# Five orders in a two-block transformer kernel: the opening's banks and loads, conv's seventh unit, the last high part in finish, the low parts around the last down result, and GpSimd's low part among its scales

## What is computed

```python
# first block, for each of 2 layers
x = x + 0.5 * swiglu(rmsnorm(x, ffn1_norm), gate, up, down)      # F = 2816
x = x + concat(sliding_window, moba, dsa attention of rmsnorm(x) @ w_in) @ w_out
x = x + 0.5 * swiglu(rmsnorm(x, ffn2_norm), gate, up, down)
# then a final rmsnorm, and the second block
x = x + post_norm(diff_attention(pre_norm(x)))
x = x + post_norm(conv_ffn(pre_norm(x)))    # (x @ w_in), causal conv of width 3, gelu(gate) * val, @ w_out
x = x + post_norm(forgetting_attention(pre_norm(x), shared k, v, gates))
x = x + post_norm(conv_ffn(pre_norm(x)))
```

## Time and profile before

| | us |
|---|---|
| median of three runs | 3137.25 |
| the profiled execution | 3136.89 |
| its span in the profile | 3135.1 |
| TensorE busy | 3085.1 |
| VectorE busy | 2095.1 |
| ScalarE busy | 1372.0 |
| GpSimd busy | 821.9 |

### The profile page before, as it was taken

How to read it: one execution, slowest core, us unless ns; L and a number is a source line. 1 busy time by engine, 2 the same in 40 slices (tenths; PEclk the granted TensorE clock), 3 DMA queues, 4 the chain that set the end, 5 groups by cost and what they waited for, 6 DMA issues and landing times.

```text
span 3135.1 us, 47847 instructions
## 1 busy us (share of the span) xinstructions
PE 3085.1 (98%) x17664; PEld 2608.0 (83%) x17664; DVE 2095.1 (67%) x3335; ACT 1372.0 (44%) x2308; POOL 821.9 (26%) x627
## 2 busy tenths in 40 slices
PE   8999999999999999999999999999999999999999
PEld 6999876898989899777899977677888886778887
DVE  6869587685958586695867753556556546576474
ACT  5535246452535353354634433644334335343242
POOL 3212346521333133264412220240000332310003
PEclk9999999999999999999999999999999999999999
DMA  4355331333334433221343333123333231223232
GB/s 125 106 148 153 102 101 41 94 102 101 104 85 115 114 88 102 77 61 54 101 121 89 103 93 96 39 61 87 107 87 100 81 96 41 68 68 109 86 99 82
DMA packets 530032, 289.14 MB, mean 92 GB/s; under 512 B 13630, under 2 KB 520225, under 8 KB 529850
## 3 DMA queue, kind: packets, MB, share of 16 engines
q1 hardware_dynamic: 527162, 281.26, 31.4%
q0 software_dynamic: 2688, 5.44, 0.5%
HBM read 284.38 MB, written 10.02 MB: 94 GB/s over the span
## 4 chain that ended last, share of the span: by engine, by line
PE 84%; DVE 7%; issue 3%; ACT 3%; POOL 1%; SPq 1%; DMA 0%; DVEq 0%; ACTq 0%; POOLq 0%
PE bank L2373 38%; PE bank L2426 24%; PE bank L2391 5%; PE bank L2679 3%; PE bank L2789 2%; PE bank L2408 2%; PE bank L2476 2%; PE bank L2831 2%; PE bank L2854 1%; PE bank L2611 1%; PE bank L2517 1%; ACT w_hi L1009 1%; DVE w_lo L1612 1%; DVE h_lo L1642 1%; DVE scaled_g L1725 0%
## 5 line engine op out<-in xcount | busy, mean ns | idle before, releaser
L1009 ACT ACTIVATE w_hi<-w_raw 128x1024 fp32r<-128x1024 f32 (+1 forms) x319 | 367.6, 1152 | 1003.4 <-PE bank L2373 612.0
L1612 DVE TENSOR_TENSOR w_lo<-w_raw,w_hi 128x1024 fp32r<-128x1024 f32 (+2 forms) x287 | 420.1, 1464 | 254.8 <-ACT w_hi L1009 254.7
L2373 PE MATMUL bank<-h_hi,w_hi 128*128 128x512 f32 (+1 forms) x1204 | 476.7, 396 | 11.5 <-DVE h_lo L1642 4.5
L2373 PE MATMUL bank<-h_hi,w_lo 128*128 128x512 f32 (+1 forms) x1204 | 469.3, 390 | 0.0
L2373 PE MATMUL bank<-h_lo,w_hi 128*128 128x512 f32 (+1 forms) x1192 | 464.8, 390 | 0.0
L2426 PE MATMUL bank<-h_hi,ws 128*128 128x256 f32 x2432 | 452.7, 283 | 0.4 <-DVE ws L1796 0.4
L2426 PEld LDWEIGHTS bank<-h_hi,ws 128*128 128x128 f32 x2432 | 385.9, 192 | 1.4 <-DVE ws L1796 0.8
L2426 PE MATMUL bank<-h_lo,ws 128*128 128x256 f32 x1216 | 344.1, 283 | 0.0
L2426 PE MATMUL bank<-t_hi,ws 128*128 128x256 f32 x1824 | 341.1, 283 | 0.0
L2373 PE MATMUL bank<-act_hi,w_hi 128*128 128x512 f32 x836 | 325.3, 389 | 0.0
L2373 PE MATMUL bank<-act_hi,w_lo 128*128 128x512 f32 x836 | 325.2, 389 | 0.0
(11 more groups left out here) (390 smaller groups left out, 6245.6 us busy)
## 6 DMA issues: line engine op xcount, KB each, us to landing
w_raw<-in_ffn_w_down_dram SPq DMA_DIRECT2D x64, 704.0 KB, 4.7
w_raw<-in_ffn_w_in_dram SPq DMA_DIRECT2D x88, 512.0 KB, 3.8
raw_g<-in_ffn_w_gate_dram SPq DMA_DIRECT2D x76, 512.0 KB, 3.9
raw_u<-in_ffn_w_up_dram SPq DMA_DIRECT2D x67, 512.0 KB, 3.8
w_raw<-in_ffn_w_out_dram SPq DMA_DIRECT2D x32, 704.0 KB, 4.6
w_raw<-in_w_in_dram SPq DMA_DIRECT2D x34, 512.0 KB, 3.8
w_raw<-in_a_w_qkv_dram SPq DMA_DIRECT2D x24, 512.0 KB, 3.8
w_raw<-in_w_out_dram SPq DMA_DIRECT2D x16, 512.0 KB, 3.9
```

What stands on the lines that cost most here:

```text
L1009: nc.scalar.activation(split_home(c)[0][:, 0:nk, 0:cols], raw[c % 2][:, 0:nk, 0:cols], ACT.Copy).then_inc(hi_ready, 1)
L1612: nc.vector.tensor_tensor(w_low[:, 0:nk, 0:cols], raw[c % 2][:, 0:nk, 0:cols], w_high[:, 0:nk, 0:cols].bitcast(f32), ALU.subtract).then_in ...
L2373: mm = nc.tensor.matmul(result(c)[0:cols, :], w[:, k, 0:cols], x[k], start=(k == 0 and n == 0), stop=(k == nk - 1 and n == 2))
```

## The change

Five orders are changed; no instruction on data is added or removed.

- **Opening.** On SyncE the load of unit 3 and the first fast load of up weights move ahead of four small loads (lam_in). On ScalarE hi(3) moves from before the third full input to before the first. In the first stage alone, VectorE does gate_whole(1) directly behind lo(4) and product_whole(1) before lo(5), with the token low parts 0 and 1 behind act_low of product 1; ScalarE does silu 1, hi(5) and the second product's high part earlier, with token_high 1 and 2 behind them. product_whole(j) for j above 0 gets a wait for act_low of the product before.
- **Conv.** In the first half, three pairs instead of two are written out ahead of the loop. ScalarE's hi(at + 2) no longer waits for made_g, which ScalarE waits for behind it; VectorE does lo(at + 2) before the division in pair 2 of the first half.
- **finish.** hi(c + 2) moves behind the last half input.
- **output_gemm.** Five input low parts, not seven, stand ahead of the last take, and three behind it.
- **Mix.** GpSimd's low part moves from before pair_scale to between its first and its second phase.

```diff
@@ fast_ff (SyncE)
-                for u in range(3 if c == 0 else 0, 2 * FAST_FROM[0]):
+                for u in range(4 if c == 0 else 0, 2 * FAST_FROM[0]):
                     load(c + u, (gate, up)[u % 2][:, :, P * (u // 2):P * (u // 2 + 1)])
-                    if c == 0 and u == 3:
-                        fast_up(name, 0, FAST_FROM[0], up)
@@ the first loads (SyncE)
+            load(3, kview(A["ffn1_w_up"], 0)[:, :, P:2 * P])
+            fast_up(stages[0], 0, FAST_FROM[0], kview(A["ffn1_w_up"], 0))
             for n, w in enumerate(("a_lam_q1_2", "a_lam_k1_2", "a_lam_q2_2", "a_lam_k2_2")):
@@ pair_scale and its loop (GpSimd)
                 for u, ph in enumerate(plan["used"]):
+                    if u == 1 and unit is not None:
+                        low(unit)
                     if ph not in plan["pool"]:
                         continue
...
-                        if MIX_Q + p + lead(name) in POOL_LOW:
-                            low(BASE[name] + MIX_Q + p + lead(name))
-                        pair_scale(name, p)
+                        later = MIX_Q + p + lead(name)
+                        pair_scale(name, p, BASE[name] + later if later in POOL_LOW else None)
@@ finish (ScalarE)
                             half_root(following, 0)
-                        if half == 1 and k == 5:
-                            hi(c + 2)
+                hi(c + 2)
                 spread_copy(following, 0)
@@ full_input (ScalarE)
-                    if name == stages[0] and k == 2:
+                    if name == stages[0] and k == 0:
                         hi(3)
@@ gated_ff (ScalarE)
                         product_high(0, 0)
+                        silu(0, 1)
+                        hi(c + 5)
+                        product_high(0, 1)
                         if early:
                             token_high(name, 1)
-                            hi(c + 5)
-                        silu(0, 1)
-                        if early:
                             token_high(name, 2)
-                        else:
-                            hi(c + 5)
-                        product_high(0, 1)
@@ conv_ff (ScalarE)
-                    lead = 2 if hf == 0 else 1
+                    lead = 3 if hf == 0 else 1
...
-                        if early:
-                            act.wait_ge(*made_g)
-                        else:
-                            hi(at + 2, jj, also=made_g)
+                        if not early:
+                            hi(at + 2, jj)
+                        act.wait_ge(*made_g)
@@ output_gemm (VectorE)
-                    for k in range(KT - 1):
+                    for k in range(KT - 3):
                         h_low(follow, k)
                 take(c + KT - 1, KT - 1)
                 if follow:
-                    h_low(follow, KT - 1)
+                    for k in range(KT - 3, KT):
+                        h_low(follow, k)
@@ gated_ff (VectorE)
+                    if j:
+                        dve.wait_ge(act_ready, FF[name] + j)
                     nc.vector.tensor_tensor(prod[:, :], gated[:, :], result(c + 1)[:, :], ALU.mult).then_inc(bank_free[1], 1)
...
                         if early:
                             lo(c + 4)
+                            gate_whole(1)
                         product_whole(0)
                         if not early:
                             lo(c + 4)
                         act_low(a0 + 1, 0)
-                        gate_whole(1)
+                        if not early:
+                            gate_whole(1)
+                            token_low(name, 0)
+                        product_whole(1)
+                        lo(c + 5)
+                        act_low(a0 + 2, 1)
                         if early:
-                            lo(c + 5)
-                        token_low(name, 0)
-                        product_whole(1)
-                        if not early:
-                            lo(c + 5)
-                        act_low(a0 + 2, 1)
+                            token_low(name, 0)
                         token_low(name, 1)
@@ conv_ff (VectorE)
-                    lead = 2 if hf == 0 else 1
+                    lead = 3 if hf == 0 else 1
...
+                        sooner = hf == 0 and isinstance(j, int) and j == 2
+                        if sooner:
+                            lo(at + 2, jj)
                         divided(at, scaled_g[:, :], jj)
-                        if not early:
+                        if not early and not sooner:
                             lo(at + 2, jj)
-                        elif not first:
+                        elif early and not first:
                             lo(at + 3)
```

More of the change, by code:

```diff
@@ L884, in sub_diagonal, with pair_scale @@
                                         ALU.mult).then_inc(sub_diag, 1)
-            def pair_scale(stage, p):
+            def pair_scale(stage, p, unit=None):
                 plan = PLAN[stage, p]
                 for u, ph in enumerate(plan["used"]):
+                    if u == 1 and unit is not None:
+                        low(unit)
                     if ph not in plan["pool"]:
```

## The result

| | before | changed |
|---|---|---|
| median of six runs, us | 3137.18 | 3158.22 (3156.79 to 3159.69) |
| profiled execution, its span | 3135.1 | 3157.3 |
| mean granted clock | 0.998 | 0.995 |

The ratio is 1.0067, with an interval of 1.0054 to 1.008. The forecast was 3139.8 with a range up to 3146: the sign of the sum was right, its size was not; the worst case that the text worked out was 3149.7.

The account below looks back on a forecast made before the run. TensorE, busy 98% of the span, was taken as the bound, so each part was priced by its standing: −3.5 − 0.7 − 0 − 4.5 + 11.2 = +2.5, giving 3139.8 us against the median, range 3131 to 3146.

Parts of the forecast that it names:

- Opening, −3.5: Opening: fast pairs start 3.5 us sooner, from 1.6 idle time, 0.8 earlier high part and 1.1 shorter token low parts.
- its gain is bounded by its idle time: Opening, VectorE's chain before the fast pairs: operations all remain, so only idle time can go, 1.6 of 2.3 us.
- lose less: Opening: VectorE's token low parts lose less beside GpSimd, which ends 2 us sooner; 1.1 us gained.
- the full inputs and GpSimd's sums come 2.1 sooner: Opening: unit 3's load issued 2.4 us sooner, so ScalarE's last full input and GpSimd's token sums come about 2.1 sooner.
- Conv, −0.7: Conv's seventh unit and the loop's pace after it (0.1 × 7.5), less loss at the next unit: −0.35 in each of two stages.
- Half hand-overs, 0: Moving the last high part in finish behind two more half inputs changes nothing: 0, ends −0.6 and +0.3.
- Hand-overs, −4.5: Taking the last down result after five input low parts removes TensorE's gaps at the stage hand-overs: −4.5 us in sum.
- the low parts of blocks 5 and 6 come 0.6 later: Hand-over mix_0 to ffn2_0: these come 0.6 later, unnoticed by TensorE, the result and last low part 1.6 us sooner.
- Mix, +11.2: GpSimd's low part behind the first scales delays TensorE by slot (one pair's turn and a unit): 5.6 us per mix stage.
- Slots 2 and 6 change nothing: Mix: in these two slots the moved low part costs and gains nothing.
- slot 5's +0.6: Mix, slot 5: like slot 4, low part between the scale phases, but with shorter queues, costs 0.6 us per stage.
- rival 1: TensorE's stand in mix slot 0 lowers its clock, 1.6 us twice: 3143.0; slot 4 too 3146.2; opening too 3146.5–3149.7; chance 0.18.

Follow-up runs that it names:

- open_order: Kernel before with the opening's new order on VectorE and ScalarE but without its moved loads; 3138.52 us against 3136.93.
- t3_dve: raw_first with the first stage's fourth token sum made by VectorE behind the pair's sums instead of by GpSimd; 3136.55 us, 1.55 under raw_first.
- mix_busy: mix_only with 11 idle matmuls on TensorE ahead of slot 0's unit in each mix stage; median 3155.99 us, 0.8 under mix_only.
- conv_only: Kernel before with only the conv edits and the one in finish; 3135.16 us against 3136.93.
- mix_only: Kernel before with only the mix edit; 3156.76 us against 3137.56, ratio 1.0059.
- slot4_only: mix_only with GpSimd's low part between the scales in slot 4 alone, ahead of them in the other slots; 3142.84 us against 3137.43.
- raw_busy: raw_first with 12 idle matmuls on a free bank in TensorE's stand before the first pair's third product; 3137.42 us, 0.7 under raw_first.
- raw_first: open_order with the low part of the first pair's weights ahead of the token low parts on VectorE in the first stage; 3138.10 us against 3136.93.

## Why the prediction was right and wrong

The forecast of the sum missed by 18.4 us. By the account by part, 10.9 of it is the mix term, 5.4 the opening and 4.4 the hand-overs, less 1.2 in conv.

**Opening, −3.5, measured +2.25: two steps failed, "its gain is bounded by its idle time" with "lose less", and that the full inputs and GpSimd's sums come 2.1 sooner.** The idle time did go, 1.5 us of it. But the chain's own work got longer, by 1.3 where I had it 1.1 shorter: unit 5's low part, the activations' two and the first two token low parts took 9.7 us before (of which the earlier trace rows has 1.48 and 3.41) and 11.0 in the fence above with the 0.92 of the first activation. I had let all but the token low parts keep their durations. The idle time was no bound, because VectorE's own work did not set when the chain ended. A subtraction of two SBUF tensors that VectorE begins inside an addition or subtraction of GpSimd's ends a fixed time behind the end of that operation, whatever stood ahead of it; closing a gap in front of it makes it begin sooner and last longer. So the pairs start 4.0 us behind GpSimd's last operation: 53.47 and 57.48 before, 54.10 and 58.10 in the changed kernel, 53.34 and 57.35 in open_order. t3_dve shows it from the other side. The Trainium skill says in "GPSIMD Engine Reference", section 1 (Specifications), that GpSimd's SBUF interfaces are shared with VectorE and that there is contention with VectorE instructions that have two SBUF inputs; the trace agrees, for the products with a bank as an operand keep their 0.66 to 0.69 beside GpSimd, and those from SBUF alone grow.

GpSimd in turn started later, 38.24 for 37.42, and not 2.1 sooner. The load was issued at 23.73 instead of 25.12, not 2.4 us sooner: it waits for a low part of its own buffer (lo_ready), a condition that its old place had hidden. It landed 8.4 us later instead of 7.4 (what lengthened it isn't shown), at 32.1, so ScalarE stood 2.10 with all eight full inputs behind it instead of six, and the root came 0.8 later, where I had it 0.8 earlier. The 3 us before the pairs that the text gave as a condition for a lower clock became 4.4, and the clock fell (0.59 over 58 to 62): the pairs start 0.6 late and are 2.1 late when it is back.

Three readings of before's trace were off. TensorE's idle times add up to 44 us with the load, not 36. The lower clock behind unit 4's stand did not lose 1.6 us of the kernel's time: in mix_busy's execution, which has the opening of before, it stayed at 1.00 there and the pairs started at 57.45 for 57.48. And the clock fell a second time in that trace, behind a stand of half the length, near the end (the timeline, then the window):

```profile
3122.58 0.80 PE L2579 MATMUL bank<-rms,ones 128*128 128x256 f32 x2 [1.53 <-DVE rms L1681]
3122.00:3126.00 4.00, 3.42 (x16) 3.27 (x17) 3.01 (x7) 1.22 (x3) 2.47 (x4) 0.63 0.00 0
```

**Conv, −0.7, measured −1.8.** The mechanism was as worked out: the bank's evacuation is the new releaser. The first stand and what comes back at the next unit are together near the forecast in conv_0 (0.53 less, 0.34 given back) and worse in conv_1 (0.18 less, 0.38 given back). Mis-sized was the pace: I had 0.75 for each stage and took most of it as lost again; it gives 0.85 and 1.1, and keeps it.

**Half hand-overs, 0.** The order in finish moved the standing of conv_0's hand-over from one block to three (0.26, 0.25 and 0.18 in conv_only for 0.26 and 0.67), and not at all in the two others. It wasn't run alone; within conv_only it is under 0.3.

**Hand-overs, −4.5, measured +0.25: the step that "the low parts of blocks 5 and 6 come 0.6 later" and the last one 1.6 sooner failed.** It took 0.82 for each low part, the mean of a row that holds one of 1.79 beside GpSimd and six of 0.74. Behind the result GpSimd makes the square and the sum of squares, 3.1 us. The low part of block 6 begins inside the square and ends 0.55 behind it, at 602.77; that of block 7 begins inside the sum and ends 0.55 behind that, at 604.46: on before's time 0.7 later than there, not 1.6 sooner. With one or two low parts behind the result, none has to wait for the sum. The hint was in the same timeline: the one low part behind the result took 0.94, not 0.74. The ffn1 to mix hand-overs, for which I had a gain of 0.15, lost 0.4 each. The further 0.35 that I added for the first unit had no row.

**Mix, +11.2, measured +19.2: the terms "Slots 2 and 6 change nothing" and slot 5's +0.6 failed, and the clock, left out of the sum.** The mechanism and its main stands were right: 3.07 for 3.15 in slot 0, slot 1's 1.08 gone, 0.63 for 0.9 in slot 3, 1.65 for 2.0 in slot 4. Slot 2 was not nothing (a stand of 0.5 and 0.9 in the two stages, for the unit's low part) and slot 5 was 1.3 instead of 0.6: there too the second phase waits behind the low part. At full clock the part made 14.4 instead of 11.2, of which 12.7 are stands. The rest is rival 1, the clock: 4.8 by mix_only's median, 5.9 in its profiled execution, 7.7 in that of the changed kernel, where it fell five times in the mix stages. It had a chance of 0.18 against the row that spoke for it, 3.18 us in the opening with a clock of 0.90 behind, which was a stand of the same length as the forecast one; the forecast should have had the clock in its likeliest case, at 1.6 twice for slot 0. Slot 4's stand of 2.3 brought it as well. By the rule of the Trainium skill that the prediction cited ("TensorE: Matmul & The Clock Gate", Part 1: The HAM clock gate), that activity is what releases the throttle, a fall behind slot 0's stand was to be expected, and the traces agree.

## What to carry to other kernels

A duration read where two engines don't overlap isn't the price where they do, and a mean over a merged row can hide both. When an edit closes one engine's gaps or moves its work behind an event that starts the other, look up when the other's operations end in that stretch: here an operation that had to wait lasted until that end and a fixed time more. Closing a gap in front of it gains nothing; moving the neighbour's end does.

A low part or a scale that stands in idle time ahead of its user isn't in the way. Moving a whole loop's order for the one iteration in which it is (slot 1, 1.08 us) cost five others (slots 0, 2, 3, 4 and 5); decide by slot. And a new stand on TensorE of the length of one that already brings its clock down has to be priced with the clock.

## What the runs showed of the hardware

VectorE's 128x512 subtraction of two SBUF tensors took 0.69 us alone and 0.92, 1.48, 1.78 and 2.89 beside different operations of GpSimd. What looks like a factor is a wait. In the trace of before, each of the 167 subtractions of 128x1024 that VectorE began inside a TENSOR_TENSOR of GpSimd's, more than 0.14 us ahead of its end, ended 1.08 to 1.09 us behind that operation's end, and they lasted 1.28 to 3.41; alone they take 1.22. The 16 input low parts of 128x512 ended 0.55 behind it, and take 0.74 alone. The same times hold in all other traces, to 0.02 us. It goes the other way as well: GpSimd's sums of 128x1024 took 2.40 when they began first, and 2.8 to 3.4 when VectorE was at work, ending 2.2 to 2.3 behind the end of VectorE's operation.

TensorE's clock fell to 1.2 GHz at every one of the 15 stands of 2.9 us and more in the 18 profiled executions (the wait for x at the start aside), and behind stands of 1.06 and 1.25 (or 1.42 and 1.25) with one group of matmuls between in both stages of the changed kernel, mix_only and slot4_only, but in neither of mix_busy. Behind shorter single stands it depends on the execution. Behind the 1.53 near the end, which all kernels have, it fell in 5 of 18; behind the 1.25 of slot 5 in 1 of 6; behind 1.6 to 2.2 before unit 4 in 2 of 6. It never fell behind the 1.78 before conv's seventh unit, or the 1.39 in raw_busy. Behind the 2.00 us stand at 16 us, which all kernels have, it fell in 12 of 18:

```profile
18.00:22.00 4.00, 3.92 (x11) 3.20 (x12) 4.00 (x7) 4.00 (x7) 0.00 (x0) 0.61 0.34 91
```

In the profiled execution of before the same window stood at 1.00. The lower clock isn't always a loss. That fall costs nothing: the six executions that have it with the opening of before are 1.1 to 1.5 us late at 30 us and within 0.3 of before's at 70 us, as the stand before unit 4 takes it up. And in raw_first it covered a wait that came next, and taking it away (raw_busy) gained 0.7 us where the windows' clocks alone would say 3.
